# The remainders of the attention operands: from GpSimd to VectorE, in the row of each task

## What is computed

```python
def gqa_attend(q, k, v):
    s = einsum("bhgqd,bhkd->bhgqk", q, k) * (HEAD_DIM ** -0.5)
    p = softmax(s, axis=-1)
    return einsum("bhgqk,bhkd->bhgqd", p, v)

def diff_attend(q, k, v, lam):
    s = einsum("bhmqd,bhmkd->bhmqk", q, k) * (DIFF_QK_DIM ** -0.5)
    p = softmax(s, axis=-1)
    w = p[:, :, 0] - lam * p[:, :, 1]
    return einsum("bhqk,bhkd->bhqd", w, v)
```

## Time and profile before

| | |
|---|---|
| time, median of 3 runs | 2867.34 us (2861.9 to 2871.57) |
| profiled execution, first to last instruction | 2869.6 us |
| the profiled execution's own time | not given apart; the span stands for it |
| PE busy (matmul) | 2368.6 us, 83% |
| DVE busy | 1712.3 us, 60% |
| ACT busy | 1051.3 us, 37% |
| POOL busy | 621.4 us, 22% |
| mean granted TensorE clock | 0.895 |
| GpSimd's remainders, line 730 | 72 instructions |

### The profile page before, as it was taken

The page is one execution under the profiler, slowest core; times in us unless marked ns, Lnnn a source line. Parts: engine busy times, 40 slices in busy tenths (PEclk is TensorE's granted clock), DMA queues, the critical chain, the costliest instruction groups (busy, mean ns, idle before and its releaser), DMA issues.

```text
span 2869.6 us, 43346 instructions
## 1 busy us (share of the span) xinstructions
PE 2368.6 (83%) x17409; PEld 2185.6 (76%) x17409; DVE 1712.3 (60%) x1905; ACT 1051.3 (37%) x1202; POOL 621.4 (22%) x637
## 2 busy tenths in 40 slices
PE   5766688979999678679999588679999958867998
PEld 4621478879999677579998587579999857757998
DVE  6599634546559645655559465555555947555554
ACT  3200223444344334343343244334344324433432
POOL 3857100020006811100008700200000860110000
PEclk9877779989999888789999798779999979978999
DMA  5277624425554432135554331134545423203452
GB/s 166 95 290 298 218 89 142 151 76 170 175 182 139 134 103 89 59 109 185 176 169 133 103 118 59 44 95 156 189 162 153 134 94 112 74 30 117 148 189 89
DMA packets 282991, 388.29 MB, mean 135 GB/s; under 512 B 7847, under 2 KB 255965, under 8 KB 276702
## 3 DMA queue, kind: packets, MB, share of 16 engines
q1 hardware_dynamic: 279148, 379.40, 40.3%
q10 hardware_dynamic: 3282, 5.74, 0.6%
q0 software_dynamic: 416, 1.08, 0.2%
HBM read 385.04 MB, written 1.05 MB: 135 GB/s over the span
## 4 chain that ended last, share of the span: by engine, by line
PE 61%; DVE 14%; POOL 13%; issue 3%; ACT 3%; POOLq 1%; DVEq 0%; ACTq 0%
PE L L752 51%; POOL rstd L716 6%; POOL work L719 6%; PE M L752 5%; DVE w_rest L349 1%; PE M L869 1%; POOL work_r L730 1%; DVE m L1906 1%; DVE gate L1906 1%; DVE m L1721 1%; DVE gate L1715 1%; DVE work L2219 1%; DVE s5z L1901 1%; PE L L896 1%; ACT w_high L343 1%
## 5 line engine op out<-in xcount | busy, mean ns | idle before, releaser
L752 PE MATMUL L<-n_high,w_high 128*128 128x256 f32 x3584 | 1051.3, 293 | 87.3 <-DVE n_rest L1659 43.7
L752 PE MATMUL L<-n_rest,w_high 128*128 128x256 f32 x3584 | 1036.2, 289 | 0.0
L752 PE MATMUL L<-n_high,w_rest 128*128 128x256 f32 x3584 | 1034.6, 289 | 0.0
L349 DVE TENSOR_TENSOR w_rest<-raw,w_high 128x2048 fp32r<-128x2048 f32 x311 | 728.0, 2341 | 388.1 <-PE L L752 339.5
L752 PEld LDWEIGHTS L<-n_high,w_high 128*128 128x128 f32 x3584 | 710.8, 198 | 111.0 <-issue 89.3
L343 ACT ACTIVATE w_high<-raw 128x2048 fp32r<-128x2048 f32 x311 | 594.0, 1911 | 479.5 <-PE L L752 427.7
L752 PEld LDWEIGHTS L<-n_rest,w_high 128*128 128x128 f32 x3584 | 711.3, 198 | 0.8
L752 PEld LDWEIGHTS L<-n_high,w_rest 128*128 128x128 f32 x3584 | 710.6, 198 | 0.0
L716 POOL TENSOR_TENSOR rstd<-work,tapc 128x256 f32 x180 | 178.0, 989 | 980.3 <-DVE work L2179 670.3
L730 POOL TENSOR_TENSOR work_r<-kv,work_r 128x512 fp32r<-128x512 f32 (+2 forms) x44 | 63.7, 1451 | 810.9 <-ACT work_r L1306 810.9
L752 PE MATMUL M<-work_r 128*128 128x256 f32 (+3 forms) x744 | 172.3, 387 | 68.6 <-POOL work_r L730 35.3
(11 more groups left out here) (341 smaller groups left out, 3035.9 us busy)
## 6 DMA issues: line engine op xcount, KB each, us to landing
raw<-in_w_in SPq DMA_DIRECT2D x116, 1024.0 KB, 5.4
raw<-in_w_ffn SPq DMA_DIRECT2D x99, 1024.0 KB, 5.2
raw<-in_w_ada SPq DMA_DIRECT2D x48, 1024.0 KB, 8.1
raw<-in_w_out SPq DMA_DIRECT2D x16, 1024.0 KB, 5.1
raw<-in_w_gate SPq DMA_DIRECT2D x11, 1024.0 KB, 5.3
raw<-in_w_up SPq DMA_DIRECT2D x11, 1024.0 KB, 5.3
raw<-in_w_down SPq DMA_DIRECT2D x11, 1024.0 KB, 5.0
raw<-in_w_four SPq DMA_DIRECT2D x6, 1024.0 KB, 4.9
```

Source lines behind the costliest of these rows:

```text
L349: nc.vector.tensor_tensor(w_rest[:, u.first % 2, :], raw[:, u.first % 4, :], w_high[:, u.first % 4, :].bitcast(F32), ALU.subtract).then_in ...
L752: ins = mm(dst, a, b, start=first and i == 0, stop=last and i == 2, skip_group_check=skip)
```

## The change

GpSimd's loop over the tasks loses the remainders; its convolution taps stay. DVE gets them in `operand_rests`: those of -1 ahead of the first `negative_max`, those of task i behind `normalise(i)` and ahead of `head_out`, `turned_rest` and the next `negative_max`. Operands, results and semaphores are the same.

```diff
@@ @block.gpsimd
             for key in TASKS:
                 if kind_of(key) == "gqa":
                     taps(FULL_OF[key[:2]], 0 if key[1] == "0" else 1)
-                for at in range(-1, len(TASKS[key])):
-                    for what, h, _, done in SPLITS[key, at]:
-                        src = operand(key, what, h)
-                        high, rest = split_of(key, what, h)
-                        pool.wait_ge(op_high, done)
-                        nc.gpsimd.tensor_tensor(rest, src, high.bitcast(F32), ALU.subtract).then_inc(op_rest, 1)
@@ attention of @block.vector
+                def operand_rests(at):
+                    for what, h, _, done in SPLITS[key, at]:
+                        src = operand(key, what, h)
+                        high, rest = split_of(key, what, h)
+                        dve.wait_ge(op_high, done)
+                        V.tensor_tensor(rest, src, high.bitcast(F32), ALU.subtract).then_inc(op_rest, 1)
                 beside, n_beside = beside_of(key)
+                operand_rests(-1)
                 negative_max(tasks[0])
                 negative_max(tasks[1])
                 for i, x in enumerate(tasks):
                     normalise(i, x)
+                    operand_rests(i)
                     if (key, i - 2) in END_OF:
                         head_out(tasks[i - 2])
```

## The result

The changed kernel takes **2883.98 us** (median of 6 runs, 2875.92 to 2890.72), the kernel before 2866.20 us beside it (6 runs, 2861.9 to 2871.57): 17.8 us more, a ratio of 1.0057 with an interval of [1.0043, 1.0071]. The forecast was 2868.4 us, range 2861 to 2877, "no change". The time lies 15.6 us above the forecast and outside its range, and 17.8 us is twice the 8.6 us that the forecast took as no change.

A forecast was written before the change was run, and what follows sets the result against it. PE's matmuls were taken to bound the kernel, filling 83% of the span, with the attentions a relay. Terms: +16.2 - 8.4 - 6.7 = +1.1 us, giving 2868.4 us, range 2861 to 2877.

The forecast's parts named there:

- Term 1: At the six gqa and diff starts, remainders behind DVE's merge and cold scores make first maxima late: 16.2 us lost.
- Term 2: Behind those starts, PE's clock returns at about the same moment, so later tasks' work runs faster: 8.4 us gained.
- Term 3: In attention rows and x merges, DVE instructions are no longer stretched beside GpSimd remainders: 4.0 us gained.
- Term 4: Remainders run faster but queue on DVE: net gains of 1.1 us in x diff, 0.4 c diff, 1.2 mem.
- Slower: the starts stay whole: At the starts PE idles again after scores 1, no clock gain, half the row gains: +12.9 us, 2880.2; chance 0.16.
- GpSimd was worse than it looks: PE's 35.3 us of waits for GpSimd shrink by half: -13.8 us, about 2853.5; chance 0.08.
- Nothing moves: Gate quarters cover the attentions, starts and rows alike, so nothing was on the path: 2867.3 us; chance 0.08.

The follow-up runs named there:

- experiment 1: Changed kernel with the remainders ahead of each attention's first task back on GpSimd, those in the rows still on DVE: 2863.93 us, 0.9987 of the kernel before.
- experiment 4: Kernel before plus 34 unread matmuls on PE behind the first two scores of each gqa and diff: 2864.87 us, ratio 0.9982.
- experiment 5: Changed kernel plus unread matmuls on PE, 44 ahead of the first scores and 8 behind them: 2870.29 us, 1.0003 of the kernel before.
- experiment 6: Kernel before plus 3 to 5 unread DVE subtractions ahead of the first maximum of each gqa and diff, remainders left on GpSimd: 2891.10 us, ratio 1.0067.
- experiment 2: Changed kernel with the rows' remainders back on GpSimd, only those ahead of each first task on DVE: 2888.77 us, 1.0073 of the kernel before.
- experiment 3: Changed kernel with the start remainders of each gqa and diff moved ahead of the merge on DVE: 2860.84 us, 0.9975 of the kernel before.
- experiment 9: Changed kernel, start remainders ahead of the merge, plus unread PE matmuls: 34 per gqa and diff, 10 in each diff's last 8 tasks: 2846.35 us, 0.9935 of the kernel before.

## Why the prediction was wrong

**Term 1, the starts: right.** 16.2 us forecast, 16.6 measured, each start within 0.1 us of its own value. The durations taken from neighbours (0.60 and 0.34 in a chain) hold. The formula that the prediction takes from the Trainium skill ("VectorE: DVE Perf Modes", section on the TRN2 errata) is stated there for an addition; single subtractions here took 0.68 and 0.42 us, so it fits them too. Charged in full within the chains (0.69 for 0.60, 0.42 for 0.34) the six starts would come 0.8 us later in sum and not 1.5. The forecast's sum did not use this.

**Term 2, what PE's clock gives back: this step failed, and its sign is wrong.** The forecast let the clock come back "some 5 us of work" after the restart, with more of the later tasks behind that moment. Already before, this held in four starts (4.8 to 5.7 us); in the two x gqa it was 6.8 and 7.4. The clock in x0's gqa, in steps of 4 us from the end of the merge; the changed kernel:

```profile
1712.27:1716.27 4.00, 2.84 (x6) 1.81 (x6) 2.38 (x6) 0.46 (x1) 0.00 (x0) 0.50 0.00 0
1716.27:1720.27 4.00, 2.62 (x8) 1.54 (x7) 1.25 (x3) 1.10 (x4) 0.00 (x0) 0.50 0.01 4
1720.27:1724.27 4.00, 4.00 (x18) 3.61 (x18) 1.94 (x4) 3.06 (x4) 0.00 (x0) 0.50 0.00 0
1724.27:1728.27 4.00, 4.00 (x15) 3.23 (x15) 2.55 (x2) 1.68 (x4) 0.00 (x0) 0.50 0.00 0
1728.27:1732.27 4.00, 3.28 (x22) 2.44 (x21) 3.08 (x8) 0.70 (x2) 0.00 (x0) 0.91 0.64 200
```

and the kernel before:

```profile
1703.53:1707.53 4.00, 1.74 (x6) 1.32 (x7) 1.92 (x5) 1.45 (x4) 0.00 (x0) 0.50 0.00 0
1707.53:1711.53 4.00, 4.00 (x17) 3.35 (x16) 1.94 (x4) 2.29 (x4) 0.00 (x0) 0.50 0.02 4
1711.53:1715.53 4.00, 3.41 (x19) 2.43 (x17) 2.17 (x2) 2.46 (x5) 0.74 (x1) 0.86 0.00 0
```

Before, the low clock ends some 9 us behind the merge; now some 16 to 17. The two scores stand alone, PE waits again (1.38 us for the multiplication of line 1735, which waits for exponentials that wait for the maxima), and only what comes after is one busy piece. Before, those scores had run ahead of the merge, so this second gap was part of one long idle time. The forecast let the cold scores count towards the clock's return and did not count the gap.

The other starts agree in sign. In the order c0, x0, x1, with gqa ahead of diff, the first low stretch ends 8.0, 16.2, 16.7, 10.6, 12.4 and 11.3 us behind the merge; before it was 7.4, 5.9, 9.1, 6.9, 9.7 and 6.9. So it ends 4.9 us later on average, where the forecast had the same moment. Counted from PE's restart behind the last gap, it is 4.4, 12.9, 11.3, 5.6, 7.0 and 6.3 us, against 5.7, 4.8, 6.8, 5.4, 7.4 and 5.3. So in four of the six the second gap fits the delay within 1.3 us. In c0's diff and x0's gqa it does not: there PE worked on at half clock for 11 to 13 us behind the gap (in x0's gqa 10.8 us without any wait, in c0's diff with one of 1.21 us), and why is open.

The Trainium skill ("TensorE: Matmul & The Clock Gate", Part 1, section "HAM oscillation — how this bites in real kernels") describes a PE that falls back to the half rate at waits that recur between short pieces of work. The trace does not show this as the cause in c0's diff. PE idles 10.7 us of it with the change (48.92 less 38.22) and 11.2 before (41.84 less 30.63), its longest wait is 2.44 us against 2.49, and yet the clock is 0.60 against 0.79.

The size of term 2 follows from experiment 1, whose rows are those of the change. There first maximum to last shrank by 10.7 us over the six against the kernel before; in the change by 11.8 - 16.6 = -4.8. So the late starts lose a further 5.9 us behind the first maximum in these profiles. By the medians it is 20.1 between the two kernels, less the 16.6, plus 0.6 by which mem is shorter in the change (25.6 and 26.1 us): 4.1. Experiments 4 and 5 give 7 to 9 (10 to 12 us less the 3.5 of the first scores), if the added matmuls do nothing but keep the clock. Term 2 was -8.4 and is +4 to +9. That error, 12 us at the least, is most of the miss of 15.6 (2883.98 less 2868.4).

**The assumption under it** was that a start is a closed piece: a clock that returns at its usual moment and an attention that goes on as before. But the low clock recurs in the rows of every diff, and where it falls changes with the start. In x0's diff the change was 3.21 us late at the eighth maximum and 0.18 at the twelfth, since the clock stayed high there; in c0's diff it was 3.88 late at the eighth and 6.82 at the twelfth, since it fell. Experiment 6 shows such a shift with no remainder moved.

**Term 3, contention gone: right in sign and place.** No 512-wide multiplication takes more than 0.49 us, and the x merges shrink from 5.0 and 5.2 us to 4.9 each. **Term 4, the queue on DVE: right.** In task 2 of x0's diff it is 5.66 us from the fourth to the fifth maximum in place of 5.99, a gain of 0.33 where 0.4 was forecast:

```profile
1825.50 0.69 DVE L1757 TENSOR_TENSOR work_r<-kv,work_r 128x512 fp32r<-128x512 f32 x1
1826.11 0.42 DVE L1757 TENSOR_TENSOR work_r<-work,work_r 128x256 fp32r<-128x256 f32 x1
...
1826.68 0.93 PE L746 MATMUL M<-work_r 64*128 64x512 f32 x3 [3.10 <-DVE work_r L1757]
```

mem gained 1.6 where 1.2 was forecast. Terms 3 and 4 were 6.7 together. Experiment 1 has 4.3 by medians with mem's start left out (5.4 of the forecast then remain), and 10.7 in the profile, so no more than their order can be confirmed.

**The rivals.** "Slower: the starts stay whole" came true in verdict and, in four starts of six, in its mechanism, with the chance of 0.16: it said that PE idles again behind scores 0 and 1 and that the busy piece counts from there, and its decision point was less than 7.6 of 15.1 us. Its 2880.2 is still 3.8 too low, since it let term 2 end at zero. Its stated sign, a fourth maximum late by as much as the first, was met in five attentions of six: 2.38, 3.61, 3.56, 2.94 and 3.86 us. The bounds of term 2, 0 and 8.4, were the true fault: a price that no row shows was bounded on the side of the gain alone, with no reason given that excludes a loss. "GpSimd was worse than it looks" wanted 17.6 us from PE's waits beside the terms; experiment 1, in which every row is on DVE and no start is late, gains 4.3 in all. "Nothing moves" fell with the first maxima.

**What stays open.** That late starts are the loss, and that a busy PE takes most of it away, is shown (experiments 1, 2, 3, 5 and 6). Why a late start moves the later low stretches as it does is not. The executions of one kernel spread over 15 us (the changed kernel), their low stretches were seen in one profile each, and no run here controls them. c0's diff is the place of the largest extra loss in two profiles (0.60 in the change, 0.57 in experiment 2, but 0.86 in experiment 5 with PE kept busy), which does not show it for all executions.

## What to carry to other kernels

Work that moves from a slow engine to a fast one loses its cover if it lands behind that engine's last obligation; put it where its input is ready and the fast engine still waits (experiment 3: the same 72 instructions, +17.8 us behind the merge, -7.4 ahead of it). Price a late first link of a relay that runs on a cold PE at more than its length, and put a loss into the bounds as well as a gain. Here 16.6 us cost 20.1 (the change against experiment 1), 11.0 us of pure delay cost 19 to 21.6 (experiment 6), and with PE kept busy 13.1 us cost some 12 (experiments 4 and 5, with terms 3 and 4 added back). Where PE waits for its relay in short gaps, matmuls that nobody reads can be worth their place, since they keep its clock (experiment 9: -20.5 us, together with the remainders ahead of the merge).

## What the runs showed that was not expected

- 11.0 us of pure delay on DVE, in six places, cost about 20 us (experiment 6); the mean clock of its profiled execution is 0.887, in the kernel before 0.895.
- With a short wait at the start of an attention the clock 16 to 24 us later is another: 0.50 there in x0's diff with the delay, 0.93 without.
- More work made the kernel faster: 34 unread matmuls per attention gained 1.8 thousandths (experiment 4), and with the remainders ahead of the merge and 80 more in the tail of each diff the whole came to 0.9935, with a good third of the gain outside the attentions in which they ran.
